# Two plain pairs of feed-forward tiles ahead of the seven-product pairs, in a two-layer encoder step

## The reference

```
x = x + mem_attend(rmsnorm(x, P['norm_mem']), mem_k, mem_v, P['mem_w_q'], P['mem_w_o'])
h = rmsnorm(x, P['norm_ffn'])
x = x + jnp.square(jax.nn.relu(h @ P['ffn_w1'])) @ P['ffn_w2']
```

## Time and profile before

| | us |
|---|---|
| median of 3 runs | 1916.02 |
| the runs | 1915.63, 1920.54, 1916.02 |
| the profiled execution, whole | 1913.13 |
| its span, first to last instruction | 1911.3 |
| PE busy in it | 1790.7 (94%) |
| DVE busy | 1163.6 (61%) |
| ACT busy | 878.8 (46%) |
| POOL busy | 283.3 (15%) |

### The profile page before, as it was taken

The page is one execution under the profiler, slowest core; times in us unless marked ns, Lnnn a source line. Parts: engine busy times, 40 slices in busy tenths (PEclk is TensorE's granted clock), DMA queues, the critical chain, the costliest instruction groups (busy, mean ns, idle before and its releaser), DMA issues.

```text
span 1911.3 us, 38165 instructions
## 1 busy us (share of the span) xinstructions
PE 1790.7 (94%) x16242; PEld 1655.9 (87%) x16242; DVE 1163.6 (61%) x2013; ACT 878.8 (46%) x1612; POOL 283.3 (15%) x238
## 2 busy tenths in 40 slices
PE   5999988999997999999999999889999799999997
PEld 5985776999887999999999667779987799999996
DVE  6677765454458766566457876655444786665553
ACT  5434556463346544444335455554433564444432
POOL 2020000200014322221100100001000342222201
PEclk9999999999998999999999999999999999999998
DMA  5200000453011223322231000133510122222321
GB/s 221 68 18 1 4 25 27 153 184 113 25 67 56 89 93 106 101 89 93 94 126 47 8 3 3 35 113 116 200 49 23 67 78 100 89 96 104 100 89 58
DMA packets 38759, 149.54 MB, mean 78 GB/s; under 512 B 4416, under 2 KB 4576, under 8 KB 36928
## 3 DMA queue, kind: packets, MB, share of 16 engines
q1 hardware_dynamic: 36288, 131.05, 20.1%
...
...
## 4 chain that ended last, share of the span: by engine, by line
PE 77%; DVE 11%; ACT 6%; issue 3%; POOL 1%; DMA 1%; DVEq 0%; ACTq 0%; SPq 0%; POOLq 0%
PE PS L808 57%; PE PS L973 14%; PE PS L985 5%; DVE wL L1845 2%; DVE wL L1849 1%; DVE hbL L2316 1%; ACT wH L1377 1%; PE PS L1233 1%; DVE stat L2210 1%; ACT hb L1377 1%; ACT hH L1377 1%; POOL sq L694 1%; DVE hL L2341 1%; DVE xT L1875 1%; ACT aP L1377 0%
## 5 line engine op out<-in xcount | busy, mean ns | idle before, releaser
L1377 ACT ACTIVATE wH<-ring 128x1024 fp32r<-128x1024 f32 (+1 forms) x302 | 263.2, 873 | 333.6 <-PE PS L808 272.4
L808 PE MATMUL PS<-hH,wH 128*128 128x272 f32 x1760 | 385.5, 301 | 33.1 <-DMA cst<-cst_in 16.7
L808 PE MATMUL PS<-hH,wL 128*128 128x272 f32 x1760 | 369.0, 291 | 0.0
L808 PE MATMUL PS<-hL,wH 128*128 128x272 f32 x1760 | 367.9, 291 | 0.0
L1849 DVE TENSOR_TENSOR wL<-ring,wH 128x1024 fp32r<-128x1024 f32 x174 | 218.8, 1258 | 183.4 <-ACT wH L1377 182.8
L808 PEld LDWEIGHTS PS<-hH,wH 128*128 128x128 f32 x1760 | 281.1, 191 | 49.1 <-issue 17.8
L973 PE MATMUL PS<-hbH,wH 128*128 128x272 f32 x896 | 262.7, 293 | 28.1 <-issue 21.8
L808 PEld LDWEIGHTS PS<-hH,wL 128*128 128x128 f32 x1760 | 280.4, 191 | 0.0
L808 PEld LDWEIGHTS PS<-hL,wH 128*128 128x128 f32 x1760 | 278.9, 190 | 0.0
L973 PE MATMUL PS<-hbH,wL 128*128 128x272 f32 x896 | 261.0, 291 | 0.0
L973 PE MATMUL PS<-hbL,wH 128*128 128x272 f32 x896 | 259.7, 290 | 0.0
...
## 6 DMA issues: line engine op xcount, KB each, us to landing
ring<-wall SPq DMA_DIRECT2D x238, 512.0 KB, 3.3
...
```

Of the source, the lines that this page charges most:

```text
L808: return e.matmul(out, lhsT=a, rhs=b, start=start, stop=stop)
L1377: return e.activation(out, in_, f, **kw)
```

## The change

The first two pairs of feed-forward tiles (4 of the 32) become plain tiles `fp` 0 to 3, each of 48 matmuls and written straight out of PSUM. The seven-product scheme starts with pair 2. `fp` tiles multiply Q11, Q12, Q21, Q22, so the residual stage now rounds these quadrants (Q12 into the new blocks `q12H`, `q12L`) and still forms the differences, but the rounding of T1, T2, T3, T4 (four instructions of 128 x 1088 on ACT, `mixed_up_hi`, and four on DVE, `mixed_up_lo`) stands behind it, in the lists for `fp` 0 to 2. `rms` moves to the third block of `fp` 1, `rstd` on ACT to the place of `fp` 1, and the weight combinations of pairs 0 and 1 on POOL go away. The 4 weight tiles are loaded either way.

```diff
-GROUPS, PAIRS = 4, 16
+GROUPS, PAIRS, PLAIN = 4, 16, 2
+SEVENS = PAIRS - PLAIN
...
-    units = up(0, M1)
-    for q in range(4):
+    units = [("fp", t) for t in range(2 * PLAIN)] + up(PLAIN, M1)
+    for q in range(PLAIN, 4):
...
+        def hid_of(n):
+
+            return n // 2, n % 2 if n // 2 < PLAIN else 1 - n % 2
...
-                add_squares(3 * l + 2, 1, 5)
-                for i in range(3):
-                    combine(l, 0, i)
-                add_squares(3 * l + 2, 6, 6)
-                combine(l, 0, 3)
-                add_squares(3 * l + 2, 7, 7)
-                for q in range(1, PAIRS):
+                add_squares(3 * l + 2)
+                for q in range(PLAIN, PAIRS):
...
+                        wait_evac(e, l, "fp", 2 * PLAIN - 1)
+                    elif q > 3:
...
+                if q == PLAIN and j in (M5, M6, M7, M4):
+                    e.wait_ge(s["f_mixed_ready"], at(l, "f_mixed_ready", (M5, M6, M7, M4).index(j) + 1))
...
-                if (q, j) == (0, M2):
-                    rms(3 * l + 2)
+
+            def up_plain(l, i):
+
+                n = tile_no(l, "fp", i)
+                e.wait_ge(w_lo, n + 1)
+                eng, v = evac_value(BEFORE[n] // NU, BEFORE[n] % NU)
+                e.wait_ge(evac[eng], v)
+                out = Q(PARITY[n])
+                for k in range(8):
+                    if i == 0:
+                        e.wait_ge(s["f_ready"], at(l, "f_ready", k + 1))
+                    if (i, k) == (1, 2):
+                        rms(3 * l + 2)
+                    w, x = weights_of(n, k), up_rows(k)
+                    for i_, (a, b) in enumerate(((0, 0), (0, 1), (1, 0))):
+                        for c in range(2):
+                            last = e.matmul(out[:, HALF_T * c:HALF_T * c + HALF_T], lhsT=w[a], rhs=x[b][c],
+                                            start=k == 0 and i_ == 0, stop=k == 7 and i_ == 2)
+                last.then_inc(pe_done, 1)
...
+                def up_hi(k):
+
+                    e.wait_ge(s["f_raw"], at(l, "f_raw", k + 1))
+                    if k >= 4:
+                        act(hbH[:, Q21:Q22 + 1, k - 4, :], hb[:, Q21:Q22 + 1, k - 4, :], ACT.Copy)\
+                            .then_inc(s["f_hi"], 1)
+                        return
+                    act(hbH[:, Q11, k, :], hb[:, Q11, k, :], ACT.Copy)
+                    act(q12H[:, k, :], hb[:, T3, k, :], ACT.Copy).then_inc(s["f_hi"], 1)
+
+                def mixed_up_hi(n):
+
+                    e.wait_ge(s["f_mixed"], at(l, "f_mixed", 8 if n else 4))
+                    b = (T1, T2, T3, T4)[n]
+                    act(hbH[:, b, :, :], hb[:, b, :, :], ACT.Copy).then_inc(s["f_mixed_hi"], 1)
...
                     up_raw(i)
+                    up_hi(i)
                     square(3 * l + 2, i)
-                    if i < 4:
-                        e.wait_ge(s["f_cross"], at(l, "f_cross", i + 1))
-                        up_hi(i, Q11, T2)
...
+                    q, m = hid_of(n)
+                    if n < 2 * PLAIN:
+                        wait_evac(e, l, "fp", n)
                     else:
-                        e.wait_ge(s["f_turn"], at(l, "f_turn", 2 * i - 7))
-                        up_hi(i, T2, Q21)
-                        e.wait_ge(s["f_turn"], at(l, "f_turn", 2 * i - 6))
-                        up_hi(i, Q21, T4 + 1)
...
+                    if st == "fp":
+                        if i < 2:
+                            mixed_up_hi(2 * i)
+                            mixed_up_hi(2 * i + 1)
+                        if i == 1:
+                            rstd(3 * l + 2)
+                        if i:
+                            squared(i - 1)
+                    elif st == "f1":
...
-                        if (q, j) == (0, M7):
-                            rstd(3 * l + 2)
...
+                def up_lo(k):
+                    e.wait_ge(s["f_hi"], at(l, "f_hi", k + 1))
+                    if k >= 4:
+                        two = [p[:, Q21:Q22 + 1, k - 4, :] for p in (hbL, hb, hbH)]
+                        tt(two[0], two[1], plain(two[2]), ALU.subtract).then_inc(s["f_ready"], 1)
+                        return
+                    tt(q12L[:, k, :], hb[:, T3, k, :], plain(q12H[:, k, :]), ALU.subtract)
+                    e.wait_ge(s["f_mixed"], at(l, "f_mixed", k + 1))
+                    tt(hbL[:, Q11, k, :], hb[:, Q11, k, :], plain(hbH[:, Q11, k, :]), ALU.subtract)\
                         .then_inc(s["f_ready"], 1)
+
+                def mixed_up_lo(n):
+                    e.wait_ge(s["f_mixed_hi"], at(l, "f_mixed_hi", n + 1))
+                    b = (T1, T2, T3, T4)[n]
+                    tt(hbL[:, b, :, :], hb[:, b, :, :], plain(hbH[:, b, :, :]), ALU.subtract)\
+                        .then_inc(s["f_mixed_ready"], 1)
...
-                        tt(x[:, T2, :], x[:, T3, :], x[:, Q11, :], ALU.subtract)
-                        tt(x[:, T1, :], x[:, T3, :], x[:, Q11, :], ALU.subtract).then_inc(s["f_cross"], 1)
-                        up_lo(i, Q11, T2, i + 1)
+                        tt(x[:, T1, :], x[:, T3, :], x[:, Q11, :], ALU.subtract).then_inc(s["f_mixed"], 1)
                     else:
-                        e.wait_ge(s["f_cross"], at(l, "f_cross", 4))
-                        tt(x[:, T2, :], x[:, Q22, :], x[:, T2, :], ALU.subtract).then_inc(s["f_turn"], 1)
+                        e.wait_ge(s["f_mixed"], at(l, "f_mixed", i - 3))
+                        link(tt(x[:, T2, :], x[:, Q22, :], x[:, T1, :], ALU.subtract))
                         tt(x[:, T3, :], x[:, Q22, :], x[:, T3, :], ALU.subtract)
-                        e.wait_ge(s["f_turn"], at(l, "f_turn", 2 * i - 7))
-                        tt(x[:, T4, :], x[:, Q21, :], x[:, T2, :], ALU.subtract).then_inc(s["f_turn"], 1)
-                        up_lo(i, T2, Q21, 2 * i - 3)
-                        up_lo(i, Q21, T4 + 1, 2 * i - 2)
+                        tt(x[:, T4, :], x[:, Q21, :], x[:, T2, :], ALU.subtract).then_inc(s["f_mixed"], 1)
+                        e.wait_ge(s["f_mixed"], at(l, "f_mixed", i + 1))
+                    up_lo(i)
...
+                    if st == "fp":
+                        if i == 0:
+                            mixed_up_lo(0)
+                            mixed_up_lo(1)
+                            e.wait_ge(s["rms_rstd"], 3 * l + 3)
+                        stt(hid[0][:, i, :], take_tile(l, "fp", i), 0.0, rs, ALU.max, ALU.mult)\
+                            .then_inc(evac["dve"], 1)
+                        if i:
+                            hid_lo(i - 1)
+                        if i in (1, 2):
+                            mixed_up_lo(i + 1)
...
-                            if q == 0:
-                                e.wait_ge(s["rms_rstd"], 3 * l + 3)
```

94 lines of the change are left out of this document (45 added, 49 removed).

## The result

| | before | after |
|---|---|---|
| the first comparison, median | 1917.64 us (4 runs, 1915.63 to 1920.54) | 1886.70 us (4 runs, 1883.82 to 1890.32) |
| ratio after / before | | 0.9848, 95% interval 0.983 to 0.9867 |
| the profiled execution, whole, and its span | 1913.13, 1911.3 | 1883.82, 1882.0 |
| all executions of the comparisons, median | 1916.0 (52, 1908.83 to 1923.53) | 1889.9 (17, 1883.82 to 1894.38) |

The change makes the kernel 1.5% faster by the first four runs and 1.4% by all. The forecast was 1896.5 with a range down to 1889.5: direction and mechanism came out, the gain is larger than forecast, and the measured 1886.7 lies 2.8 us under the range. The median of all 17 executions is 0.4 us inside its lower edge.

What follows compares the result with a forecast made beforehand. PE, 94% busy, waits for the residual stage on DVE and ACT. Per layer 25.7 + 0.7 + 0.95 + 1.4 = 28.7 us against 38.3 and 38.6, 19.5 less: 1916.0 - 19.5 = 1896.5 us, range 1889.5 to 1903.5.

Steps and rivals of the forecast that it cites:

- The slow clock: Behind M6's wait in the kernel before: granted clock 0.50, 18 matmuls taking 4.2 us in place of 2.3.
- The stretch to pair 2's M5: From the end of `mo` on PE to pair 2's M5: 28.7 us per layer, against 38.3 and 38.6 before.
- wait at block 7 of `fp` 0: PE waits about 0.95 us in `fp` 0 for the last residual block, wanted after 42 matmuls; ends 0 and 2.
- wait of `fp` 2 for `rs`: `fp` 2 wants `fp` 0's bank, which DVE reads only with `rs`: a wait of 1.4 us, ends 0.5 and 3.
- `rms` and restarts: The four matmuls of `rms`, 0.92 us, cost PE about 0.7 more than the starts they displace.
- The residual stage: DVE and ACT during `mo`: residual steps of 5.35 us for i < 4 and 5.9 after, in place of 7.4.
- Behind it: After `fp` 2's wait for `rs`: no further wait reaches PE and the clock has no stop like the 9.7 us one.
- (a): Residual stage: POOL doesn't get in DVE's way or DVE is first, so block 7's wait goes; 1894.5 us, 14%.
- (b): Residual stage: DVE first, POOL second, the split delayed; steps of 5.55 and 6.0, `rs` 0.9 later; 1898.5 us, 12%.
- (c): Pairs 2 to 4 give time back: PE's 2.1 us of idle time doubles in both layers; 1900.7 us, 9%.
- (d): The wait is moved, not removed: M6 of pair 2 waits for ACT's copy of M1; 1919.7 us, 4%.
- (e): `fp` 0 already waits for the whole residual stage, 6.2 us in place of 0.95; 1907 us, 3%.

Runs made afterwards that it cites:

- a_round_in_stage: The changed kernel with T1 to T4 rounded and split inside the residual stage again, plain tiles kept; 1898.73 us, ratio 0.9909 to the kernel before.
- b_filled2: The kernel before with 72 unused matmuls per layer ahead of every wait of M6 of pair 0, filling PE's idle time; 1912.58 us, ratio 0.998.
- a_small_adds: The changed kernel with POOL's additions of squares for the feed-forward norm cut to one column, which makes the norm wrong; median 1888.4 us.
- a_plain1: The changed kernel with one plain pair in place of two, 12 matmuls fewer per layer, T3 and T4 rounded later; median 1895.4 us.

## Why the prediction was right and wrong

**What bounds the kernel.** Right. PE's stop at M6 of pair 0, ended by the residual stage, is gone with the change, and a_round_in_stage brings a stop of 5.0 us back when the roundings return. The prediction didn't see that POOL's combinations stretched one step of the old stage to 9.8 us; it compared with three steps of 7.4, but used neither number in its sum.

**The slow clock.** The 1.9 us per layer of the earlier trace rows were counted in the stretch before as if they were lost. b_filled2 shows that they were covered by M7's wait for the copy behind `rs`. The total isn't touched, since the stretch was measured as a whole, but filling the wait in the old kernel would have gained nothing in that part.

**The stretch to pair 2's M5.** Forecast 28.7, measured 28.71 and 28.73. Its terms were less exact than the sum. The prediction counted its waits from start to start, so the measured ones are counted in the same way; the idle times of the timeline, 0.62 and 1.10, begin 0.16 us later, at the matmul's shown end.

| term | forecast | measured, layer 0 |
|---|---|---|
| 204 matmuls | 25.7 | 25.7 |
| wait at block 7 of `fp` 0 | 0.95 | 582.79 - 576.74 - 42 x 0.1258 = 0.77 |
| wait of `fp` 2 for `rs` | 1.4 | 591.86 - 590.47 - 0.13 = 1.26 |
| `rms` and restarts | 0.7 | 28.71 - 25.66 - 0.77 - 1.26 = 1.0 |

590.47 is the last start of `fp` 1. The `rms` term was too small because its four matmuls displace none: the next product stands 0.9 behind the earlier trace rows, all of it extra, and a first matmul behind a stop takes 0.07 to 0.1 longer. Two waits 0.3 too long together made up for it, so that the sum came out to 0.1 is luck.

**The residual stage.** Right to 0.1: steps of 5.34 and 5.81 against 5.35 and 5.9. `rs` was ready 51.5 us behind the first residual, against 51.7 in the forecast, and by the table loads' rows alone, with no drain between them, as the earlier trace rows had it.

**Behind it.** This is the step that failed. It said "No wait that I can find reaches PE" and looked only for new waits. In the sum it took the old ones, 2.1 us idle between 612 and 760, as given and so put their change at nothing. They hung on work that the change moves: the squares and splits of two hidden tiles in each pair. Measured: 1.75 + 2.04 us less, with 0.17 + 0.18 less up to the end of `mo` besides (not looked into). The 4.1 us in all make 19.5 into 23.6. The prediction named this as a possible larger gain, gave it 5% and put 2 us of it into its low end; rows of the kernel before, the same two waits in pair 2 and again in pair 3, would have given its size.

**The base.** The forecast went from the median of three runs, 1916.0, and allowed 2.9 us for the difference from the profiled execution. That was too little: at identical instructions the kernel after has spans outside the two parts that differ by 9 us. With 23.6 from 1916.0 the forecast would have been 1892.4. Repeats gave 1889.7, 1892.9 and 1890.8; the first four runs, at 1886.7, were lower still, with a mean clock of 0.988 against 0.9868 over all 17, which is chance. Of the pooled difference 2.5 us lie outside the two parts, some 1.6 of them clock by the estimate above.

**The rivals.** (a) was wrong for this kernel and right as a price, by a_small_adds. (b): POOL was first, so its steps of 6.0 didn't come. (c): pairs 2 to 4 gave time and took none; three hidden tiles were done before pair 2 began, and not four left waiting for it. (d) didn't occur with two plain pairs; in a_plain1 a wait of 1.7 us moved to M7 of the first seven-product pair. (e): the wait at block 7 is 0.62, so `fp` 0 doesn't wait for the whole stage.
